# A hybrid attention block on one core: split products whose high and low token halves stream as one operand, and four fp32 matmuls as rounded pairs

## What is computed

```python
h = rmsnorm(x, norm_attn)
proj = h @ w_in                      # queries, keys, values, gates
o_nsa = nsa_attention(...)           # bias table rel_bias, compressed / selected / window
o_sb = stick_breaking_attention(...)
mixed = merge0 * (o_nsa @ w_up_nsa) + merge1 * (o_sb @ w_up_sb)
x = x + mixed @ w_out
h = rmsnorm(x, norm_mlp)             # mean of squares over the features
x = x + square(relu(h @ w_ff1)) @ w_ff2     # 1024 -> 4096 -> 1024
return rmsnorm(x, norm_final)
```

## Time and profile before

| | |
|---|---|
| three runs | 784.09, 781.94, 784.12 us; median 784.09 |
| the profiled execution | 782.67 us, its span 780.8 us |
| PE | 770.2 us busy (99%) |
| PE, weight loads | 650.1 us |
| DVE | 461.1 us busy (59%) |
| ACT | 387.9 us busy (50%) |
| POOL | 277.5 us busy (36%) |

### The profile page before, as it was taken

The page is one execution under the profiler, slowest core; times in us unless marked ns, Lnnn a source line. Parts: engine busy times, 40 slices in busy tenths (PEclk is TensorE's granted clock), DMA queues, the critical chain, the costliest instruction groups (busy, mean ns, idle before and its releaser), DMA issues.

```text
span 780.8 us, 11862 instructions
## 1 busy us (share of the span) xinstructions
PE 770.2 (99%) x4292; PEld 650.1 (83%) x4292; DVE 461.1 (59%) x936; ACT 387.9 (50%) x719; POOL 277.5 (36%) x366
## 2 busy tenths in 40 slices
PE   8999999999999999999999999999999999999996
PEld 6878888888877777778888888999999999999895
DVE  7446557787757676635544737556665556664334
ACT  6333314688966576574345644344444444443321
POOL 1255424511112332146455644333333322233640
PEclk9999999999999999999999999999999999999998
DMA  7954013210150110134232223332222333332213
GB/s 261 340 180 163 1 55 101 88 54 29 35 155 28 55 55 29 55 108 148 95 108 98 91 101 115 109 108 88 85 93 88 108 109 109 108 108 81 87 49 109
DMA packets 26006, 77.82 MB, mean 100 GB/s; under 512 B 3710, under 2 KB 6966, under 8 KB 25695
## 3 DMA queue, kind: packets, MB, share of 16 engines
q1 hardware_dynamic: 23868, 74.72, 29.0%
q10 hardware_dynamic: 2083, 2.37, 1.0%
HBM read 73.90 MB, written 2.13 MB: 97 GB/s over the span
## 4 chain that ended last, share of the span: by engine, by line
PE 93%; DVE 4%; ACT 2%; DMA 1%; issue 1%; DVEq 0%; ACTq 0%
PE bank L1508 31%; PE bank L1914 20%; PE bank L1888 5%; PE bank L1886 5%; PE bank L1884 5%; PE bank L1820 2%; PE bank L1802 2%; PE bank L1734 2%; PE bank L1859 2%; PE bank L1858 2%; PE bank L1854 2%; PE bank L1779 2%; PE bank L1752 1%; PE bank L1520 1%; PE bank L1521 1%; PE bank L1522 1%
## 5 line engine op out<-in xcount | busy, mean ns | idle before, releaser
L644 POOL TENSOR_TENSOR wlo<-wraw,whi 128x256 fp32r<-128x256 f32 x344 | 262.8, 796 | 461.4 <-ACT whi L685 378.6
L685 ACT ACTIVATE whi<-wraw 128x1024 fp32r<-128x1024 f32 x77 | 80.6, 1053 | 32.0 <-PE bank L1914 19.1
L1508 PE MATMUL bank<-hh,wlo 128*128 128x512 f32 x304 | 81.0, 396 | 0.7 <-DVE gm L1202 0.6
L1508 PE MATMUL bank<-hl,whi 128*128 128x512 f32 x304 | 80.6, 392 | 0.0
L1508 PE MATMUL bank<-hh,whi 128*128 128x512 f32 x304 | 79.6, 391 | 0.0
L1508 PEld LDWEIGHTS bank<-hh,whi 128*128 128x128 f32 x304 | 56.6, 188 | 11.7
L1508 PEld LDWEIGHTS bank<-hl,whi 128*128 128x128 f32 x304 | 56.4, 188 | 11.7 <-issue 0.2
L1508 PEld LDWEIGHTS bank<-hh,wlo 128*128 128x128 f32 x304 | 55.4, 188 | 12.8 <-DVE gm L1202 0.9
L1914 PE MATMUL bank<-r_l,whi 128*128 128x512 f32 x224 | 57.9, 390 | 0.0
L1914 PE MATMUL bank<-r_h,wlo 128*128 128x512 f32 x224 | 56.3, 392 | 0.0
L1914 PE MATMUL bank<-r_h,whi 128*128 128x512 f32 x224 | 55.7, 389 | 0.0
(11 more groups left out here) (310 smaller groups left out, 1647.1 us busy)
## 6 DMA issues: line engine op xcount, KB each, us to landing
wraw<-in_panels SPq DMA_DIRECT2D x101, 512.0 KB, 3.3
land<-in_panels SPq DMA_DIRECT2D x12, 512.0 KB, 4.5
w1k<-in_w SPq DMA_DIRECT2D x1, 2048.0 KB, 9.3
w1v<-in_w SPq DMA_DIRECT2D x1, 2048.0 KB, 14.8
svraw<-in_panels SPq DMA_DIRECT2D x4, 512.0 KB, 5.3
hank<-bias_by_distance SPq DMA_DIRECT2D x4, 512.0 KB, 6.3
x_res<-in_xT SPq DMA_DIRECT2D x4, 512.0 KB, 4.4
out_dram<-x_res SPq DMA_DIRECT2D x12, 128.0 KB, 1.8
```

The lines of the kernel that those rows point to most:

```text
L644: ins = nc.gpsimd.tensor_tensor(wlo[:, s, k:k + 2], wraw[s][:, k:k + 2], whi[:, s, k:k + 2].bitcast(F32), ALU.subtract)
L685: A(whi[:, s], wraw[s][:], ACT.Copy).then_inc(w_hi, 1)
L1508: ins = M(b[:, cols], lhs, (xl if a == 1 else xh)[:, row + k, cols], start=(m == 0), stop=(m == 23))
```

## The change

`h2h` and `h2l` become the two parts of one tile `h2`, and `th` and `tl` of one tile `tt`. In `products` the high weights stream the high and the low tokens as one operand of 512 columns (two pieces of 256): the high part's result goes into the near half of the bank and the low part's into the far half. The low weights by the high tokens stay 4 matmuls of 256 columns. What is read out of a bank is now the sum of its two halves, and DVE gets the additions. The four fp32 matmuls become pairs of float32r matmuls, with copies and subtractions that make the pairs.

```diff
-            def products(o, wh, wl, xh, xl, start, stop):
+            def products(o, wh, wl, x, start, stop):
                 for k in range(4):
-                    M(o, wl[:, k], xh[:, k], start=(start and k == 0), stop=False, skip_group_check=True)
+                    M(o[:], wh[:, k], x[:, :, k], start=(start and k == 0), stop=False, skip_group_check=True)
                 for k in range(4):
-                    M(o, wh[:, k], xl[:, k], start=False, stop=False, skip_group_check=True)
-                for k in range(4):
-                    ins = M(o, wh[:, k], xh[:, k], start=False, stop=(stop and k == 3), skip_group_check=True)
+                    ins = M(o[:, 0:T // 2], wl[:, k], x[:, 0, k], start=False, stop=(stop and k == 3), skip_group_check=True)
...
-                pe_.wait_ge(u2_copied, j + 1)
+                pe_.wait_ge(u2_made, j + 1)
...
             def c11(j):
+                a, x, t = bank[j % 2], bank[2], tmp[:, 0, near]
+                dve.wait_ge(x_copied, j + 1)
+                emptied(V.tensor_tensor(t, x[:, far], t, ALU.add), ("wx", j))
                 stored(dve, ("wx", j))
-                V.tensor_tensor(tmp[:, 0, near], bank[j % 2][:, near], tmp[:, 0, near], ALU.add).then_inc(c11_made, 1)
-                dve.wait_ge(c11_made, j + 1)
-                positive(tmp[:, 0, near], tmp[:, 0, near], near)
+                V.tensor_tensor(t, a[:, near], t, ALU.add).then_inc(c11_made, 1)
+                dve.wait_ge(c11_made, 2 * j + 1)
+                V.tensor_tensor(t, a[:, far], t, ALU.add).then_inc(c11_made, 1)
+                dve.wait_ge(c11_made, 2 * j + 2)
+                positive(t, t, near)
+            def m7_low(j):
+                t = tmp[:, 1, far]
+                dve.wait_ge(m7_copied, j + 1)
+                V.tensor_tensor(t, bank[3][:, far], t, ALU.add).then_inc(c22_made, 1)
+            def u2(j):
+                dve.wait_ge(u2_copied, j + 1)
+                V.tensor_tensor(u2s[:], bank[j % 2][:, far], u2s[:], ALU.add).then_inc(u2_made, 1)
...
             def c22(j):
                 dve.wait_ge(v_ready, j + 1)
+                dve.wait_ge(c22_made, 3 * j + 1)
+                V.tensor_tensor(t, a[:, near], t, ALU.add).then_inc(c22_made, 1)
+                dve.wait_ge(c22_made, 3 * j + 2)
+                V.tensor_tensor(t, a[:, far], t, ALU.add).then_inc(c22_made, 1)
...
+            def c12_high(j):
+                A(tmp[:, 0, T // 2:T], result(act, ("wa", j))[:, 0:T // 2], ACT.Copy).then_inc(c12_copied, 1)
...
             def c12(j):
-                a = result(dve, ("wa", j))
-                emptied(positive(tmp[:, 0, far], a[:, near], far), ("wa", j))
+                dve.wait_ge(c12_copied, j + 1)
+                emptied(V.tensor_tensor(t, bank[j % 2][:, far], t, ALU.add), ("wa", j))
+                stored(dve, ("wa", j))
+                positive(t, t, far).then_inc(pos1, 1)
             def c21(j):
-                emptied(V.tensor_tensor(tmp[:, 1, near], r[:, near], u2s[:], ALU.add), ("wr", j))
+                V.tensor_tensor(t, r[:, near], u2s[:], ALU.add).then_inc(c21_made, 1)
+                dve.wait_ge(c21_made, j + 1)
+                emptied(V.tensor_tensor(t, r[:, far], t, ALU.add), ("wr", j))
...
-                filled(M(b[0:H, :], relx[:], oneh[:, T * i:T * i + T], start=True, stop=True), f"vec{i}")
+                for part in (1, 0):
+                    ins = M(b[0:H, :], relx_r[:, part], oneh_r[:, T * i:T * i + T], start=(part == 1), stop=(part == 0))
+                filled(ins, f"vec{i}")
...
-            filled(M(b[:], ones[:], sqs[:], start=True, stop=True), "rms")
+            for part in (1, 0):
+                ins = M(b[:], ones_r[:], sqs_r[:, part], start=(part == 1), stop=(part == 0))
+            filled(ins, "rms")
...
+            act.wait_ge(sqs_done, KT)
+            A(sqs_r[:, 0], sqs[:], ACT.Copy).then_inc(sqs_hi, 1)
+            act.wait_ge(table_in, 16 * 3)
+            A(oneh_r[:], oneh[:], ACT.Copy).then_inc(table_hi, 1)
...
+            act.wait_ge(x_ss, KT)
+            A(x_ss_r[:, 0], mx[0][:], ACT.Copy).then_inc(x_ss_hi, 1)
...
             V.tensor_tensor(tr[:, T3], h2raw[:, 4:8, far], h2raw[:, 0:4, far], ALU.subtract).then_inc(hx_raw, 1)
+            dve.wait_ge(x_ss_hi, 1)
+            V.tensor_tensor(x_ss_r[:, 1], mx[0][:], x_ss_r[:, 0].bitcast(F32), ALU.subtract).then_inc(x_ss_lo, 1)
```

More of the change, by code:

```diff
@@ L329, in block_kernel @@
         dts = place("dts", [55, H, P], at=at_sbq + 6144)
+        relx_r = place("relx_r", [BUCKETS + 1, 2, H], F32R, at=at_sbq + 14080)
+        oneh_r = place("oneh_r", [BUCKETS + 1, 2 * T], F32R, at=tmp_at)
+        sqs_r = place("sqs_r", [P, 2, T], F32R, at=at_sbq)
         relx = place("relx", [BUCKETS + 1, H], at=at_sbq + 10240)
@@ L342, in block_kernel @@
         svraw = [place(f"svraw{c}", [P, 8, P], at=at_g + 4096 * c) for c in range(RING)]
+        ones_r = place("ones_r", [P, P], F32R)
         kd1 = place("kd1", [P, 2, T], F32R, at=tmp_at)
@@ L385, in block_kernel @@
         mx = [place(f"mx{i}", [P, T], at=at_sbk + 16384 + 2048 * i) for i in range(4)]
+        x_ss_r = place("x_ss_r", [P, 2, T], F32R, at=at_sbk + 16384 + 2048)
         x_res = place("x_res", [P, KT, T], at=at_sbk)
-        h2h = place("h2h", [P, KT, T], F32R, at=at_q)
-        h2l = place("h2l", [P, KT, T], F32R, at=at_q + 16384)
+        h2 = place("h2", [P, 2, KT, T], F32R, at=at_q)
+        h2h, h2l = h2[:, 0], h2[:, 1]
         r_h = place("r_h", [P, 2 * 8, T], F32R, at=at_sbv)
@@ L935, in _ @@
                 act.wait_ge(r_lo, 8 + 2 * j - 1)
-                emptied(A(tmp[:, 0, 0:T // 2], result(act, ("wx", j))[:, 0:T // 2], ACT.Copy), ("wx", j))
+                A(tmp[:, 0, 0:T // 2], result(act, ("wx", j))[:, 0:T // 2], ACT.Copy).then_inc(x_copied, 1)
                 act.wait_ge(s3_used, j + 1)
@@ L1008, in _ @@
                     V.tensor_tensor(sqs[:], sqs[:], sqt[:, k % 2], ALU.add).then_inc(sqs_done, 1)
+            dve.wait_ge(sqs_hi, 1)
+            V.tensor_tensor(sqs_r[:, 1], sqs[:], sqs_r[:, 0].bitcast(F32), ALU.subtract).then_inc(sqs_lo, 1)
+            dve.wait_ge(table_in, 16 * 3)
+            dve.wait_ge(set_done, 4)
+            V.tensor_copy(relx_r[:, 0], relx[:]).then_inc(table_lo, 1)
+            dve.wait_ge(table_lo, 1)
+            V.tensor_tensor(relx_r[:, 1], relx[:], relx_r[:, 0].bitcast(F32), ALU.subtract).then_inc(table_lo, 1)
             def bias_half(i):
@@ L1438, in _ @@
                 c11(j)
+                m7_low(j)
                 sum_low(j, S1)
@@ L1443, in _ @@
                     first_sums(j + 1)
+                u2(j)
+                if j + 1 < N_SEVEN:
                     third_sum(j + 1)
@@ L1875, in _ @@
             b = claim(pe_, "rms2")
-            pe_.wait_ge(x_ss, KT)
-            filled(M(b[:], ones[:], mx[0][:], start=True, stop=True), "rms2")
+            pe_.wait_ge(x_ss_lo, 1)
+            for part in (1, 0):
+                ins = M(b[:], ones_r[:], x_ss_r[:, part], start=(part == 1), stop=(part == 0))
+            filled(ins, "rms2")
             for n in range(2, 8):
                 panel(P_FF + n, ("ff", 0, n), h2h, h2l)
-            def products(o, wh, wl, xh, xl, start, stop):
+            def products(o, wh, wl, x, start, stop):
                 for k in range(4):
-                    M(o, wl[:, k], xh[:, k], start=(start and k == 0), stop=False, skip_group_check=True)
+                    M(o[:], wh[:, k], x[:, :, k], start=(start and k == 0), stop=False, skip_group_check=True)
                 for k in range(4):
-                    M(o, wh[:, k], xl[:, k], start=False, stop=False, skip_group_check=True)
-                for k in range(4):
-                    ins = M(o, wh[:, k], xh[:, k], start=False, stop=(stop and k == 3), skip_group_check=True)
+                    ins = M(o[:, 0:T // 2], wl[:, k], x[:, 0, k], start=False, stop=(stop and k == 3), skip_group_check=True)
                 return ins
```

59 lines of the change are left out of this document (33 added, 26 removed).

## The result

The changed kernel takes 776.96 us (median of 5 runs, 776.76 to 777.37), the kernel before 782.36 beside it (5 runs, 781.27 to 784.12). The ratio is 0.9926, with an interval of 0.9910 to 0.9941: 5.8 us by the ratio, where I had summed 5.4. The profiled execution took 777.13 us, with a span of 775.3 (before: 782.67 and 780.8).

What follows compares the result with a forecast made beforehand. The prediction took PE's instructions to bound the kernel. Block products (3.4 us) and fp32 pairs (1.95) summed to 5.4 us less, with added work hidden: 778.0 us, between 777.3 and 778.7, range 775.3 to 781.0.

Steps and rivals of the forecast that it cites:

- What bounds: Whole kernel: PE busy 770.2 of 780.8 us, longest wait 1.1 us, so the kernel is as long as PE's instructions.
- The block products: Feed-forward stage, 84 products: each 1.387 us instead of 1.44, a round 20.74 instead of 21.02, 3.4 us saved over twelve rounds.
- Rival 1: Block products: a two-piece 512-column matmul costs 0.24 us, like two matmuls; about 782.4 us, no change; 6 in 100.
- pairs of switches: Feed-forward stage: each pair of changes of matmul width costs PE 0.02 us; a round goes from three pairs to seven.
- The fp32 pairs: `rms`, two bias calls and `rms2`: a float32r pair takes 0.454 us, saving 3 x 0.50 + 0.45 = 1.95 us.
- The cover: DVE's seven additions a round and ACT's copy stay hidden behind PE at every place checked, and cost nothing.
- `u2`: Ahead of `S1`: the new addition ends about 592.6, PE wants it at 594.05; slack 1.4 us, smallest in the round.
- `c22`: Ahead of `S4`: now two additions, from 595.74 to 596.6, against PE at 598.29; slack 1.6 us.
- `c11`: Ahead of `S2`: with five more additions and ACT's copy it ends at 587.8, against 589.93; slack 2 us.
- the slack of `land`: Transfer into `land`: moved at most 0.9 us, to 590.6, where `first_sums` wanted it at about 590.7; slack used up.
- At the start and at `rms2` the covers: Start: pair ready at 25.5, PE at 26.54; one-hot slack 0.9 us. `rms2`: ready by 437.2, PE at 441.50. No cost.
- The level: Profiled execution 782.67 less 5.4 gives 777.3, the median 784.09 gives 778.7; 778.0 was said in between.

Runs made afterwards that it cites:

- E1: Changed kernel with each 512-column matmul of a block product issued as two of 256 columns: 780.46 us, ratio 0.9970 to the kernel before.
- E3: Changed kernel with 512- and 256-column matmuls in turn inside a block product, not four and four: 778.99 us, one run.
- E4: Changed kernel with the first bias call's weights widened from 8 to 128 columns and the second's two table waits removed: 776.57 us, one run.
- E5: Changed kernel with the operands of both bias calls padded with zeros from 33 to 128 rows: 776.57 us, one run.
- E6: Changed kernel with four useless dependent 128x128 multiplications on DVE ahead of `u2` in each round: 780.13 us, ratio 0.9974 to the kernel before.
- E7: Changed kernel with nine useless dependent 128x128 multiplications on DVE ahead of `u2` in each round: 817.82 us, ratio 1.0469 to the kernel before.
- E9: Changed kernel with two dependent 128x128 multiplications on DVE ahead of `u2` in each round: 777.03 us, ratio 0.9925 to the kernel before.
- E11: Same kernel as E8, run again beside the unedited changed kernel (776.92 us): 777.18 us.
- E8: Changed kernel with bias operands padded to 128 rows, `T4`'s low weights first, seven last panels as 8 matmuls of 512 and 8 of 256 columns: 776.84 us.

## Why the prediction was right

**What bounds.** PE, as read. Where PE does not wait, the changed kernel's span moved by what PE's own instructions moved (5.3 us busy, 5.5 us span).

**The block products.** The prices of 0.120 and 0.2268 us hold, for the two-piece operand too: 4 x 0.2268 + 4 x 0.120 = 1.387, and 1.38 was measured. Rival 1 (0.24 us for such a matmul) is dead by the same row. E1 shows that the four matmuls less are the cause. The term was 3.4 us and measured 3.7: seven pairs of switches cost 20.71 - 20.60 = 0.11 us in a round and not 0.14, 0.016 each, and E3 shows that a price for each switch was too simple a picture. The fixed part of 2.5 ns in the Trainium skill (TensorE: Matmul & The Clock Gate, Back-to-back issue gap) would have given 0.8 us ahead of the switches, an estimate from that page; the 3.7 us measured speak for the 13 ns of the rows.

**The fp32 pairs** are the term that was mis-sized: 1.95 predicted, 1.65 measured. I took 0.454 for a bias pair "whose rows are 33 partitions", with the words "I take the same". Both the change to 33 rows and the one back cost 0.10 us, since the load is not made ahead; `rms` bears the first (0.56), the bias pair the second. E4 ruled out the waits and the narrow weights, E5 the rest. The trace of the kernel before had the sign: its bias load starts with the matmul at 27.49 too, behind 0.76 us of idleness, and `rms` cost 0.95 where `rms2`, with no bias call behind it, cost 0.91.

```profile
27.49 0.10 PEld L1608 LDWEIGHTS bank<-oneh,relx 33*8 33x8 f32 x2 [0.76 <-issue]
```

The two errors, 0.3 us more in the stage and 0.3 less in the pairs, cancelled in the sum of 5.4. That the sum came out so near was luck, the mechanism was not.

**The cover.** `u2`: slack 1.4 predicted, 1.47 in the rows, and E6, E7 and E9 find its edge there. `c22`: 1.6 predicted, 594.74 - 593.07 = 1.67. I was too cautious at two places. `c11` ends at 583.21 and `S2` starts at 586.48, 3.3 us of slack and not 2 (3.7 from the last reading of the bank, at 582.76, which is all that PE waits for). I had put all five additions between the low part and the end of `c11`. Those of `c12` and `c21` stand ahead of the low part, where DVE had idle time before, and `m7_low` stands behind `c11`: against the `S3` product the low part starts 0.35 us later than before, and two additions more follow it. And the slack of `land`, which I called used up, is 1.2 us: issued at 581.53, it lands at most 4.6 us later, at 586.1, and `first_sums` starts at 587.29 with no idle time ahead of it. At the start and at `rms2` the covers held: `sqs_r` is ready at 25.5 for 26.42, `x_ss_r` at 436.3 for 440.17. Bank 3 is free at 598.64 for the `S3` product at 600.32, and after the rounds the last low part ends at 725.51 for PE at 727.06, 1.55 us against the 1.5 predicted.

**The level.** The sum made on the profiled execution gave 777.3, and its counterpart took 777.13. The half of the 1.4 us between that execution and the median of before, which made it 778.0, was noise: five runs of before have a median of 782.36.

## What to carry to other kernels

When PE never waits, count its instructions: at the same number of columns each matmul less was worth 13 ns here, and two halves in different places can be streamed as one operand at no extra cost. Before work is given to another engine, look for the smallest slack between its chain and the bound engine's need; here 0.5 us more was free and 1.6 us more cost 3 to 4 us, since a round repeats twelve times. A short matmul with fewer rows than its neighbours costs about 0.1 us on either side of it, so zero rows up to the neighbours' number are worth a trial, with an eye on what fills them.

## What the runs showed of the hardware that I had not expected

A load of 33-row weights behind a matmul of 128 rows is not made ahead, nor the next of 128 rows behind the 33, while a second one of 33 is: 0.10 us for each change; weights of 33 rows by 128 columns made it 0.66 us for the pair and not 0.56.

The multiplications of 128x128 on DVE in E6, E7 and E9 have two lengths. In E6 the first three start 0.32 us apart and the fourth takes 0.72 us:

```profile
592.11 0.72 DVE L1443 TENSOR_TENSOR ones_r<-ones 128x128 fp32r<-128x128 f32 x1
```
```profile
591.90 3.81 POOL L652 TENSOR_TENSOR wlo<-wraw,whi 128x256 fp32r<-128x256 f32 x4 [11.04 <-ACT whi L693]
```

The fourth starts while a subtraction of POOL is running. The whole stage shows the same: in E6 11 of 48 and in E7 44 of 108 start so, and each of them takes 0.69 to 0.72 us; all others take 0.28 or 0.29. E9's pair ends ahead of POOL's row. `u2`, which reads a bank, takes 0.41 or 0.42 us beside POOL too. That POOL holds them up is what the rows suggest; no run moves POOL's work, so it is not shown.

The first 14 us vary by more than the late edits are worth, and partly by PE's clock. The matmuls of 512 columns start 0.43 us apart there, which is 512 columns at 1.2 GHz, and later 0.23. In the changed kernel the granted clock (the last column but two) says the same, 0.50 from 8.5 to 11.4 us with PE at work throughout; ahead of that PE had stood three times, for 1.0, 0.2 and 0.3 us. The step to 0.23 stands at 11.8 us there, in E11 at 11.9, in E8 at 13.6, with PE at work without a wait since 8.7 in both of the last. E8 starts `rms` 27.79 - 27.00 = 0.8 us later than E11, and 1.7 us at half speed are 0.85. E8's own view reads 1.00 over all this time, against the spacing of the matmuls: that trace has no record of the clock before 13.7 us. Where the two differ, go by the spacing. The changed kernel's view, then E8's timeline of PE and its view:

```profile
8.50:11.40 2.90, 2.90 (x8) 1.83 (x7) 2.31 (x4) 2.10 (x5) 1.35 (x1) 0.50 1.05 414
```
```profile
11.43 0.63 PE L1617 MATMUL bank<-hl,whi 128*128 128x512 f32 x1
11.86 0.63 PE L1609 MATMUL bank<-hh,whi 128*128 128x512 f32 x1
...
13.56 0.47 PE L1613 MATMUL bank<-hh,wlo 128*128 128x512 f32 x1
13.87 0.39 PE L1617 MATMUL bank<-hl,whi 128*128 128x512 f32 x1
```
```profile
0.00:13.60 13.60, 10.57 (x32) 8.37 (x33) 11.26 (x16) 9.24 (x13) 5.57 (x8) 1.00 0.87 321
```
